# A state-space scan woven into a matmul stream: gate product in tile pieces, chunk splits moved to other rounds, DMA issues moved between queues

## The chip, the cores and the metric

The kernel runs on one core of one Trainium2 chip. The metric is the device time of one execution in microseconds (us), the median of three. Engines are named PE (matrix engine), DVE (vector), ACT (scalar), POOL (GpSimd) and SP (the queue that issues most transfers).

## What is computed

Two transformer-like blocks over 512 tokens of width 1024, in float32. The first block (retention, pooling, a convolutional feed-forward) and the last parts (attention, feed-forwards) are not touched. The change lies in the state-space mixer of the second block:

```python
u = (h @ w_in).reshape(bsz, seq, 64, 16)
bu = einsum('gnk,lgk->lgn', b, u)             # complex, 64 states per group
x  = associative_scan(combine, a, bu)         # x[l] = a * x[l-1] + bu[l]
y  = einsum('gkn,lgn->lgk', c, x) + d * u     # real part
z  = gelu(y)
val, gate = split(z @ w_glu, 2)
x  = x + val * sigmoid(gate)
```

## The kernel before

Every float32 product with a weight is made of three matmuls: the weight and the activation are each split into a high and a low part, and high*high, high*low and low*high are added in one PSUM bank. Weights come in **chunks** of 512 KB through a ring of six buffers (`RING`): SP issues the load of chunk n once chunk n-6 is used up, ACT writes the high part (L1161, `w_hi`), POOL the low part (L1012, `w_lo`), and PE waits for both in `take_chunk`. Where the weights have a gain, ACT first scales the chunk (L1156).

The stage of interest runs from about 621 to 749 us. PE first makes `u` for the first half of the columns (`("u", 0)`, L397 to L399), then for the second half tile by tile (`("u", 1)`, L428 to L430): four token tiles times four chunks, 16 slots of six matmuls. Beside these, 16 **rounds** of the scan run, one per batch of four groups. Rounds 0 to 5 sit in the slots that `round_in` names, rounds 6 to 15 follow. Round b is, on each engine in program order:

- PE: transpose the inputs of batch b+1 (`s5_states`, L712, bank `ut`), input product of batch b (`s5_inc`, L723, bank `sv`), output of batch b-2 (`s5_out`, L735 and L739, bank `y`), at some rounds a transpose back (`s5_turn_back`, L747, bank `zt`, where `back_in` says so), and from round 6 six matmuls of the gate product (`gate_rows`, L766 to L768).
- ACT: at the rounds of `made_in` the high part of one gate chunk (L1161); `u_t` of b+1 (L1383); the swapped state `sv_sw` (L1396, L1397); gelu of b-2 (L1391); the high part of what was turned back (L1170); the swapped `zs_sw` of b (L1405, L1406), which waits for DVE's `zs`.
- DVE: two products from the `sv` bank (L2079, L2080), `zc` of b-1 plus `zs_sw` (L2069, this frees PE's `s5_out(b-1)`), in rounds after those of `back_in` the low part (L1582, `a_lo`), then the subtraction with `sv_sw` (L2087), the scan (L2089), `zc` (L2097) and `zs` (L2098). The next round's ACT part hangs on this `zs`.
- POOL: the low parts of the gate chunks, and between them the decay tables `r_c` (L1001) that the scan reads. `decays_from` writes their order out: tables 0 to 5 before gate chunk 0's low part, 6 before chunk 1's, 7 to 10 before chunk 2's, 11 and 12 before chunk 3's, 13 to 15 after it. In this text gate chunks 0 to 3 are those of the first gate product `("glu_g", 0)`.

The gate product holds four PSUM banks; the other four go round among `ut`, `sv`, `y` and `zt`, so each bank is reused after four openings. A bank `zt` is free when DVE has made its low part.

The matrices of the scan (records, 544 KB and 256 KB per batch) were stored to DRAM earlier and are loaded again through four buffers (`RECS`): the first two by ACT, the next two and all later ones by SP between chunk loads, in the order that `next_records` writes out.

Of the kernel before, what the change touches and what calls it, by code (L numbers as in the profile page):

```python
# [85 lines left out]
def program(nc, x, w_in, w_pool, pool_scale, w_out, ln1_g, ln1_b, w_up, conv_w, conv_b, w_down, ln2_g, ln2_b,  # L86
# [7 lines left out]
    with ExitStack() as ctx:  # L94
# [226 lines left out]
        def _(pe):  # L321
# [431 lines left out]
            def gate_rows(k, tiles):  # L753

                j = k // 2
                if j not in gate_parts:
# [4 lines left out]
                wh, wl = gate_parts[j]
                pe.wait_ge(lo_ready, turned + k + 1)
                for t in tiles:
                    s = slice(t * P, t * P + P)
                    o = gate_banks[t]
                    pe.matmul(o, a_hi[:, k, s], wh[:, k % 2, :], start=(k == 0), stop=False)  # L766
                    pe.matmul(o, a_hi[:, k, s], wl[:, k % 2, :], start=False, stop=False)
                    m = pe.matmul(o, a_lo[:, k, s], wh[:, k % 2, :], start=False, stop=(k == KT - 1))  # L768
                    if k == KT - 1:
                        over = close_bank(("glu_g", 0, t), m)  # L770
                if k == KT - 1:
# [248 lines left out]
        def _(sp):  # L1020
# [58 lines left out]
            def stores_landed():  # L1079

                for i in range(2):
                    sp.wait_ge(st_out[i], 16 * (NB // 2))
                    sp.wait_ge(k_out[i], 16 * (NB // 2) * T)
                sp.wait_ge(e_out, 16 * NB)

            def load_attention_constants():

                for dst, src in ((hg[:, 0:ROPE], mla_k_rope_norm_2), (hg[:, ROPE:], mla_q_rope_norm_2[0]),
                                 (frq[:, :], c_freq)):
                    sp.dma_start(dst, src.partition_broadcast(P)).then_inc(m_in, 16)  # L1090
                for i, src in enumerate((mla_q_nope_norm_2[0], mla_k_nope_norm_2)):
                    sp.dma_start(gcol[0:NOPE, i:i + 1], src.rearrange("(e a) -> e a", a=1)).then_inc(m_in, 16)
                sp.dma_start(mask[:, :], c_mask).then_inc(m_in, 16)
                sp.dma_start(pos_i[:, :], positions_2[0].rearrange("(t p) -> p t", p=P)).then_inc(m_in, 16)
# [1221 lines left out]
```

## Time and profile before

| | |
|---|---|
| median of 3 runs | 1798.78 us (1798.54 to 1799.17) |
| the profiled execution | 1799.17 us, span 1797.3 us |
| PE busy | 1747.7 us, 97% of the span |
| DVE, ACT, POOL busy | 45%, 37%, 39% |
| stretch of the scan rounds | about 650 to 740 us |
| first matmul after the last gate matmul | 748.59 us |

The profile is of one execution. The timeline view gives instructions in order of time: start, duration, engine, line, operation, what is written from what, and in brackets the idle time of the engine before it with what ended it. The windows view gives busy time and granted clock of a stretch.

### The profile page before, as it was taken

Reading aid. Unit: us, or ns where it says so; the run is one execution under the profiler, and the core shown is the slowest. Engines: PE = TensorE matmul, PEld = TensorE weight load, DVE = VectorE, ACT = ScalarE, POOL = GpSimd, SP = SyncE. Lnnn points to the kernel's source line nnn. Section 1 sums busy time; section 2 is a strip of 40 time slices with the busy share of each in tenths; the row PEclk is TensorE's granted clock in tenths of the full one; section 3 lists DMA queues with packets and bytes.
Section 4 is the critical chain, followed back from the end, with each engine's and each line's share of the span. In section 5 each row is a group of like instructions: output and inputs, shape, how many; then the busy total and the mean of one; then the engine's idle time right before and its main releaser. Section 6 shows DMA issues by size and latency. Waiting matters only on the chain.

```text
span 1797.3 us, 22686 instructions
## 1 busy us (share of the span) xinstructions
PE 1747.7 (97%) x9006; PEld 1454.5 (81%) x9006; DVE 817.4 (45%) x1398; ACT 665.5 (37%) x1128; POOL 704.5 (39%) x331
## 2 busy tenths in 40 slices
PE   8999999899999899999999999999999999999999
PEld 6887977788788687789888888888888888888887
DVE  3876899779957637333211111138665311111111
ACT  3433234234244556524322313276654332122221
POOL 4432243534444232433453444433801345344442
PEclk9999999999999899999999999999999999999999
DMA  9422224353535367323333233222200233332332
GB/s 239 96 82 82 72 85 152 106 154 118 162 111 157 117 201 255 112 71 106 101 99 95 88 100 99 85 79 64 71 1 25 83 96 102 95 94 94 95 99 77
DMA packets 242280, 189.61 MB, mean 105 GB/s; under 512 B 41472, under 2 KB 199296, under 8 KB 242176
## 3 DMA queue, kind: packets, MB, share of 16 engines
q1 hardware_dynamic: 240304, 182.80, 34.1%
q10 hardware_dynamic: 1872, 5.37, 0.9%
q8 instruction: 72, 1.18, 0.3%
q14 instruction: 32, 0.26, 0.0%
HBM read 168.74 MB, written 19.40 MB: 105 GB/s over the span
## 4 chain that ended last, share of the span: by engine, by line
PE 82%; DVE 11%; ACT 3%; issue 2%; DMA 1%; POOL 1%; DVEq 0%; SPq 0%; ACTq 0%
PE ps L371 12%; PE ps L373 12%; PE ps L372 12%; PE ps L397 9%; PE ps L398 9%; PE ps L399 9%; PE ps L428 3%; PE ps L430 3%; PE ps L429 3%; PE ps L873 2%; PE ps L854 2%; PE ps L864 1%; DVE x_rows L1676 1%; ACT w_hi L1161 1%; PE ps L846 1%
## 5 line engine op out<-in xcount | busy, mean ns | idle before, releaser
L1012 POOL TENSOR_TENSOR w_lo<-w_raw,w_hi 128x1024 fp32r<-128x1024 f32 (+3 forms) x283 | 668.2, 2371 | 1032.2 <-ACT w_hi L1161 1032.1
L371 PE MATMUL ps<-a_hi,w_hi 128*128 128x512 f32 (+1 forms) x1184 | 442.5, 374 | 4.3 <-POOL w_lo L1012 4.3
L373 PE MATMUL ps<-a_hi,w_lo 128*128 128x512 f32 (+1 forms) x1184 | 440.5, 372 | 0.0
L372 PE MATMUL ps<-a_lo,w_hi 128*128 128x512 f32 (+1 forms) x1184 | 440.3, 372 | 0.0
L1161 ACT ACTIVATE w_hi<-w_raw 128x1024 fp32r<-128x1024 f32 (+3 forms) x283 | 284.9, 1018 | 214.8 <-DMA w_raw<-in_ffn_w_gate_up_dram 71.2
L371 PEld LDWEIGHTS ps<-a_hi,w_hi 128*128 128x128 f32 x1184 | 223.0, 188 | 45.5 <-issue 7.2
L373 PEld LDWEIGHTS ps<-a_hi,w_lo 128*128 128x128 f32 x1184 | 223.0, 188 | 38.9
L372 PEld LDWEIGHTS ps<-a_lo,w_hi 128*128 128x128 f32 x1184 | 223.1, 188 | 38.3
L2141 DVE TENSOR_TENSOR ev<-ps,xh 128x512 f32<-128x512 f32 x44 | 30.4, 691 | 411.9 <-PE ps L373 383.0
L397 PE MATMUL ps<-w_hi,h_hi 128*128 128x512 f32 x476 | 189.6, 398 | 8.7 <-DVE x_rows L1648 4.9
L398 PE MATMUL ps<-w_lo,h_hi 128*128 128x512 f32 x476 | 188.5, 396 | 0.0
L399 PE MATMUL ps<-w_hi,h_lo 128*128 128x512 f32 x476 | 188.4, 396 | 0.0
L1646 DVE TENSOR_TENSOR x_rows<-ps,x_rows 128x512 f32<-128x512 f32 x72 | 49.1, 690 | 224.8 <-PE ps L399 193.8
L1177 ACT ACTIVATE h_hi<-ev 128x512 fp32r<-128x512 f32 x66 | 41.5, 629 | 209.7 <-DVE ev L2141 195.5
L397 PEld LDWEIGHTS ps<-w_hi,h_hi 128*128 128x128 f32 x476 | 90.1, 189 | 32.0 <-issue 10.6
L397 PE MATMUL ps<-w_hi,a_hi 128*128 128x512 f32 (+1 forms) x288 | 113.2, 393 | 1.8 <-DVE a_lo L1582 1.8
L398 PE MATMUL ps<-w_lo,a_hi 128*128 128x512 f32 (+1 forms) x288 | 112.3, 390 | 0.0
L399 PE MATMUL ps<-w_hi,a_lo 128*128 128x512 f32 (+1 forms) x288 | 112.2, 390 | 0.0
L399 PEld LDWEIGHTS ps<-w_hi,h_lo 128*128 128x128 f32 x476 | 90.1, 189 | 21.2
L398 PEld LDWEIGHTS ps<-w_lo,h_hi 128*128 128x128 f32 x476 | 90.1, 189 | 20.7
L1260 ACT ACTIVATE xh<-ps 128x512 f32<-128x512 f32 x44 | 26.3, 598 | 166.2 <-PE ps L373 166.2
L428 PE MATMUL ps<-w_hi,a_hi 128*128 128x512 f32 (+2 forms) x208 | 77.4, 372 | 5.7 <-POOL w_lo L1012 2.4
(346 smaller groups left out, 2382.8 us busy)
## 6 DMA issues: line engine op xcount, KB each, us to landing
w_raw<-in_ffn_w_gate_up_dram SPq DMA_DIRECT2D x88, 512.0 KB, 3.8
w_raw<-in_w_up_dram SPq DMA_DIRECT2D x44, 512.0 KB, 3.9
w_raw<-in_ffn_w_down_dram SPq DMA_DIRECT2D x40, 512.0 KB, 3.7
w_raw<-in_w_in_dram SPq DMA_DIRECT2D x20, 512.0 KB, 4.3
w_raw<-in_w_down_dram SPq DMA_DIRECT2D x20, 512.0 KB, 4.3
s_records<-stage SPq DMA_DIRECT2D x16, 544.0 KB, 5.2
w_raw<-in_ssm_w_glu_dram SPq DMA_DIRECT2D x16, 512.0 KB, 3.7
rec<-s_records SPq DMA_DIRECT2D x14, 544.0 KB, 5.1
```

The costliest lines, as they stand in the source:

```text
L371: pe.matmul(bank, wh, xh_, start=first, stop=False)
L372: pe.matmul(bank, wh, xl_, start=False, stop=False)
L373: return pe.matmul(bank, wl, xh_, start=False, stop=last)
L397: pe.matmul(o, ah[:, k + kk, s], wh[:, kk, :], start=(n == 0 and kk == 0), stop=False)
L398: pe.matmul(o, ah[:, k + kk, s], wl[:, kk, :], start=False, stop=False)
L399: m = pe.matmul(o, al[:, k + kk, s], wh[:, kk, :], start=False, stop=end)
L428: pe.matmul(o, ah[:, k + kk, s], wh[:, kk, :], start=(k + kk == 0), stop=False)
L429: pe.matmul(o, ah[:, k + kk, s], wl[:, kk, :], start=False, stop=False)
L430: m = pe.matmul(o, al[:, k + kk, s], wh[:, kk, :], start=False, stop=end)
L1012: pool.tensor_tensor(w_lo[:, n % RING, 0:w], w_raw[:, n % RING, 0:w], w_hi[:, n % RING, 0:w].bitcast(F), ALU.subtract).then_inc(lo_made, 1)
L1161: act.activation(w_hi[:, n % RING, 0:w], w_raw[:, n % RING, 0:w], ACT.Copy).then_inc(hi_made, 1)
L1646: ins = v.tensor_tensor(o, b, o, ALU.add)
```

## The change

Four things are changed together.

- `gate_rows(k, tiles)`, one k-row at a time for a pair of tiles, becomes `gate_piece(j, tiles)`: both k-rows of one chunk for one tile. It starts at round 7 instead of 6, and waits once per chunk for the low part of the second k-row (for the last chunk, for the first and then the second). The order after round 15 is written anew.
- `back_in` has its first entry at round 5 instead of 4; `made_in` has the gate chunks at rounds 5, 6, 10 and 12 instead of 3, 7, 11 and 13. `decays_from` stays.
- `s5_states(0)` is issued before the first matmul of `("u", 1)` instead of inside it.
- ACT issues the loads of all four first records and of seven small attention constants; SP no longer issues these, and its later record loads follow one another in another order (`next_record`).

```diff
-        back_in = {4: 0, 6: 1, 8: 2, 10: 3, 12: 4, 14: 5}
+        back_in = {5: 0, 6: 1, 8: 2, 10: 3, 12: 4, 14: 5}
-        made_in = {3: 1, 7: 2, 11: 3, 13: 4}
+        made_in = {5: 1, 6: 2, 10: 3, 12: 4}
...
-            def gate_rows(k, tiles):
-
-                j = k // 2
+            def gate_piece(j, tiles):
+
                 if j not in gate_parts:
                     if not held:
                         gate_banks.extend(open_bank(("glu_g", 0, t)) for t in range(TT))
                         held.extend(bank_no["glu_g", 0, t] % 8 for t in range(TT))
+                    pe.wait_ge(lo_ready, turned + 2 * j + 2 - (j == TT - 1))
                     gate_parts[j] = take_chunk(rows_of(ssm_w_glu_2[0], 2 * j, 2, D, HALF), 2, HALF)
                 wh, wl = gate_parts[j]
-                pe.wait_ge(lo_ready, turned + k + 1)
-                for t in tiles:
-                    s = slice(t * P, t * P + P)
+
+                def row(t, kk):
+                    k, s = 2 * j + kk, slice(t * P, t * P + P)
                     o = gate_banks[t]
...
+                if j < TT - 1:
+                    for t in tiles:
+                        row(t, 0)
+                        m = row(t, 1)
+                    if tiles[-1] == TT - 1:
+                        chunk_over(m)
+                else:
+                    for t in tiles:
+                        row(t, 0)
+                    pe.wait_ge(lo_ready, turned + KT)
+                    for t in tiles:
+                        over = close_bank(("glu_g", 0, t), row(t, 1))
                     chunk_done.append(over)
...
-                if b_ >= 6:
-                    gate_rows((b_ - 6) // 2, (0, 1) if b_ % 2 == 0 else (2, 3))
+                if b_ >= 7:
+                    gate_piece((b_ - 7) // TT, [(b_ - 7) % TT])
+
+            s5_states(0)
 
             def beside_rows(t, n):
-                if TT * t + n == 1:
-                    s5_states(0)
...
             s5_out(NB - 2)
+            gate_piece(2, [1, 2])
+            s5_out(NB - 1)
             s5_turn_back(KT - 2)
-            gate_rows(KT - 3, range(TT))
-            s5_out(NB - 1)
+            gate_piece(2, [3])
             s5_turn_back(KT - 1)
-            gate_rows(KT - 2, range(TT))
-            gate_rows(KT - 1, range(TT))
+            gate_piece(3, range(TT))
...
-            def next_records(b_):
-                if b_ >= 2:
-                    sp.wait_ge(*closed(("y", b_ - 2)))
-                    load_out_part(sp, b_ - 2 + RECS)
-                if b_ + RECS < NB:
-                    sp.wait_ge(zs_ready, b_ + 1)
-                    load_state_part(sp, b_ + RECS)
+            def next_record(b_):
+                sp.wait_ge(zs_ready, b_ + 1)
+                load_state_part(sp, b_ + RECS)
+                sp.wait_ge(*closed(("y", b_)))
+                load_out_part(sp, b_ + RECS)
...
-                for later, rounds in ((5, range(0, 4)), (7, range(4, 5)), (9, range(5, 10)), (10, range(10, NB - 2))):
+                for later, records in ((RING - 1, range(0, 2)), (RING + 1, range(2, 3)), (RING + 3, range(3, NB - RECS))):
...
-            for b_ in range(2):
+            for b_ in range(RECS):
                 load_state_part(act, b_)
                 load_out_part(act, b_)
+            for dst, src in ((hg[:, 0:ROPE], mla_k_rope_norm_2), (hg[:, ROPE:], mla_q_rope_norm_2[0]),
+                             (frq[:, :], c_freq)):
+                act.dma_start(dst, src.partition_broadcast(P)).then_inc(m_in, 16)
...
             s5_gelu(NB - 2)
+            s5_gelu(NB - 1)
             split(("zt", KT - 2), *turned_back(KT - 2))
-            s5_gelu(NB - 1)
```

## Rows read from the trace of the kernel before

**Rows 1.** The page: span, and one line of its DMA issues.

```profile
span 1797.3 us, 22686 instructions
...
rec<-s_records SPq DMA_DIRECT2D x14, 544.0 KB, 5.1
```

**Rows 2.** Windows view: stretch, its length, busy PE, PEld, DVE, ACT, POOL; PEclk; DMA.

```profile
690.00:700.00 10.00, 8.69 (x78) 6.99 (x74) 7.45 (x14) 5.76 (x14) 3.88 (x4) 0.83 0.59 206
```

**Rows 3.** Timeline of PE: end of `("u", 0)`, and the first wait in `("u", 1)`.

```profile
640.40 0.39 PE L397 MATMUL ps<-w_hi,a_hi 128*128 128x512 f32 x1
...
645.84 0.39 PE L428 MATMUL ps<-w_hi,a_hi 128*128 128x512 f32 x1
...
652.59 0.47 PE L428 MATMUL ps<-w_hi,a_hi 128*128 128x512 f32 x1 [0.45 <-POOL w_lo L1012]
```

**Rows 4.** Timeline of ACT ahead of the rounds; ACTq is its queue of transfers.

```profile
628.33 0.45 ACTq L932 DMA_DIRECT2D rec<-s_records  x1
...
647.10 0.59 ACT L1374 ACTIVATE u_c<-ps 64x512 f32<-64x512 f32 x1 [1.04 <-DVE u_c L2058]
```

**Rows 5.** Timeline of DVE: the scans of rounds 4, 5 and 6.

```profile
678.18 0.69 DVE L2089 TENSOR_TENSOR_SCAN z<-r_c,z 128x256 f32<-128x256 f32 x1
...
684.70 0.69 DVE L2089 TENSOR_TENSOR_SCAN z<-r_c,z 128x256 f32<-128x256 f32 x1
...
689.06 0.69 DVE L2089 TENSOR_TENSOR_SCAN z<-r_c,z 128x256 f32<-128x256 f32 x1
```

**Rows 6.** Timeline of DVE in round 7, and the scans of rounds 8, 9 and 15.

```profile
691.59 0.42 DVE L2069 TENSOR_TENSOR zc<-zc,zs_sw 128x256 f32<-128x256 f32 x1
692.05 1.08 DVE L1582 TENSOR_TENSOR a_lo<-ps,a_hi 128x512 fp32r<-128x512 f32 x1
693.89 1.47 DVE L2087 TENSOR_TENSOR z<-z,sv_sw 128x256 f32<-128x256 f32 x1 [0.76 <-ACT sv_sw L1397]
695.71 0.78 DVE L2089 TENSOR_TENSOR_SCAN z<-r_c,z 128x256 f32<-128x256 f32 x1 [0.35 <-POOL r_c L1001]
...
700.23 0.69 DVE L2089 TENSOR_TENSOR_SCAN z<-r_c,z 128x256 f32<-128x256 f32 x1
...
704.72 0.69 DVE L2089 TENSOR_TENSOR_SCAN z<-r_c,z 128x256 f32<-128x256 f32 x1
...
735.85 0.69 DVE L2089 TENSOR_TENSOR_SCAN z<-r_c,z 128x256 f32<-128x256 f32 x1
```

**Rows 7.** Source view of L2087: instructions and durations in ns (min/median/max).

```profile
L2087 DVE TENSOR_TENSOR z<-z,sv_sw x16: 412/426/1472, 653.6 to 735.4; 128x256 f32<-128x256 f32 x16
```

**Rows 8.** Timeline of ACT and POOL in round 7.

```profile
691.58 1.06 ACT L1161 ACTIVATE w_hi<-w_raw 128x1024 fp32r<-128x1024 f32 x1
692.54 0.37 ACT L1383 ACTIVATE u_t<-ps 128x256 f32<-128x256 f32 x1
...
692.72 2.35 POOL L1012 TENSOR_TENSOR w_lo<-w_raw,w_hi 128x1024 fp32r<-128x1024 f32 x1 [13.14 <-ACT w_hi L1161]
```

**Rows 9.** Timeline of PE: start of round 8, then the tail after round 15.

```profile
693.19 0.46 PE L712 MATMUL ps<-ident,u_c 64*128 64x64 f32 x4 [1.31 <-DVE a_lo L1582]
693.57 1.10 PE L723 MATMUL ps<-u_t,rec 128*128 128x64 f32 x8
...
738.95 0.34 PE L735 MATMUL ps<-rec,u_t 128*64 128x64 f32 x4
...
740.58 0.66 PE L747 MATMUL ps<-ident,y_c 128*128 128x128 f32 x4 [0.48 <-ACT y_c L1391]
...
745.74 0.50 PE L766 MATMUL ps<-w_hi,a_hi 128*128 128x512 f32 x1 [1.60 <-DVE a_lo L1582]
...
748.59 0.39 PE L397 MATMUL ps<-w_hi,a_hi 128*128 128x512 f32 x1
```

**Rows 10.** Timeline of ACT in the tail.

```profile
740.54 2.96 ACT L1161 ACTIVATE w_hi<-w_raw 128x1024 fp32r<-128x1024 f32 x3
743.40 1.10 ACT L1170 ACTIVATE a_hi<-ps 128x512 fp32r<-128x512 f32 x1
```

More of the change, by code:

```diff
@@ L759, in gate_rows @@
                         held.extend(bank_no["glu_g", 0, t] % 8 for t in range(TT))
+                    pe.wait_ge(lo_ready, turned + 2 * j + 2 - (j == TT - 1))
                     gate_parts[j] = take_chunk(rows_of(ssm_w_glu_2[0], 2 * j, 2, D, HALF), 2, HALF)
                 wh, wl = gate_parts[j]
-                pe.wait_ge(lo_ready, turned + k + 1)
-                for t in tiles:
-                    s = slice(t * P, t * P + P)
+                def row(t, kk):
+                    k, s = 2 * j + kk, slice(t * P, t * P + P)
                     o = gate_banks[t]
[L766 to L771, printed above, removed]
+                    pe.matmul(o, a_hi[:, k, s], wh[:, kk, :], start=(k == 0), stop=False)
+                    pe.matmul(o, a_hi[:, k, s], wl[:, kk, :], start=False, stop=False)
+                    return pe.matmul(o, a_lo[:, k, s], wh[:, kk, :], start=False, stop=(k == KT - 1))
+                if j < TT - 1:
[10 more added lines that the diff above has]
+                        over = close_bank(("glu_g", 0, t), row(t, 1))
                     chunk_done.append(over)
-                elif k % 2 and tiles[-1] == TT - 1:
-                    chunk_over(m)
             def s5_round(b_):
@@ L1077, in store_batch @@
                                      e_t[:, :, GB * i:GB * i + GB, :]).then_inc(e_out, 16)
[L1079 to L1094, printed above, removed]
-            def next_records(b_):
-                if b_ >= 2:
-                    sp.wait_ge(*closed(("y", b_ - 2)))
-                    load_out_part(sp, b_ - 2 + RECS)
-                if b_ + RECS < NB:
-                    sp.wait_ge(zs_ready, b_ + 1)
-                    load_state_part(sp, b_ + RECS)
+            def next_record(b_):
[3 more added lines that the diff above has]
+                load_out_part(sp, b_ + RECS)
             for n, (src, kn, cn, _) in enumerate(chunk_src):
@@ L1112, in _ @@
                         store_batch(f)
-                if n == chunks_at[("u", 1, 0)] + 3:
-                    stores_landed()
-                    for b_ in range(2, RECS):
-                        load_state_part(sp, b_)
-                        load_out_part(sp, b_)
-                for later, rounds in ((5, range(0, 4)), (7, range(4, 5)), (9, range(5, 10)), (10, range(10, NB - 2))):
-                    if n == chunks_at[("u", 1, 0)] + later:
-                        for b_ in rounds:
-                            next_records(b_)
-                if n == chunks_at[("u", 1, 0)] + 13:
-                    load_attention_constants()
+                for later, records in ((RING - 1, range(0, 2)), (RING + 1, range(2, 3)), (RING + 3, range(3, NB - RECS))):
+                    if n == chunks_at[("u", 1, 0)] + later:
+                        for b_ in records:
+                            next_record(b_)
+            for i in range(2):
+                sp.wait_ge(st_out[i], 16 * (NB // 2))
+                sp.wait_ge(k_out[i], 16 * (NB // 2) * T)
+            sp.wait_ge(e_out, 16 * NB)
             for half in range(2):
@@ L1366, in _ @@
             act.wait_ge(e_out, 16 * NB)
-            for b_ in range(2):
+            for b_ in range(RECS):
                 load_state_part(act, b_)
                 load_out_part(act, b_)
+            for dst, src in ((hg[:, 0:ROPE], mla_k_rope_norm_2), (hg[:, ROPE:], mla_q_rope_norm_2[0]),
+                             (frq[:, :], c_freq)):
+                act.dma_start(dst, src.partition_broadcast(P)).then_inc(m_in, 16)
+            for i, src in enumerate((mla_q_nope_norm_2[0], mla_k_nope_norm_2)):
+                act.dma_start(gcol[0:NOPE, i:i + 1], src.rearrange("(e a) -> e a", a=1)).then_inc(m_in, 16)
+            act.dma_start(mask[:, :], c_mask).then_inc(m_in, 16)
+            act.dma_start(pos_i[:, :], positions_2[0].rearrange("(t p) -> p t", p=P)).then_inc(m_in, 16)
             def odd_rows(half, j):
```

## The prediction, made before the changed kernel was run

> **What bounds the kernel now.** I read the page first: PE is busy for 97% of the span [rows 1], so the question is only where PE waits, and whether a wait moves. The windows of ten us over the scan stage come next. In the worst of them PE is busy 8.69 of 10 us, and its granted clock is 0.83 [rows 2]. With the two levels of 2.4 and 1.2 GHz, a mean of 0.83 is (1 - 0.83) / 0.5 x 10 = 3.4 us at the lower one. Then I read the timelines engine by engine. The reader should see three things there.
>
> First, `("u", 1)` is set by PE itself: six matmuls a slot, 24 of them from 640.40 to 645.84, that is 0.227 us each, with one wait of 0.45 us at 652.59 [rows 3].
>
> Second, from round 5 on, the scan sets the pace. One scan follows the other by 4.36 us in round 6 (684.70 to 689.06) and by 4.49 us in round 9, both without a gate chunk, but by 6.65 us in round 7 (689.06 to 695.71) [rows 5, 6]. Round 7 has a chunk in front: ACT's `w_hi` comes 2.52 us after the scan of round 6, before `u_t` and `sv_sw`, for which DVE waits; POOL's `w_lo` starts 1.14 us after that and ends at 695.07 [rows 8]. DVE's subtraction starts at 693.89, takes 1.47 us instead of the usual 0.43, ends 0.29 us after POOL's pass, and the scan then waits 0.35 us for its table [rows 6, 7]. Rounds 7, 11 and 13 look so, 2.2 us longer than the others each.
>
> Third, after the scan of round 15 (735.85) a chain leads to the next product at 748.59, 12.74 us later: `y` of batch 15 at 738.95, gelu, three `w_hi` of the next product at 740.54, the last turned-back high part at 743.40, its low part, and PE at 745.74 after 1.60 us of waiting [rows 9, 10].
>
> **The change part by part.** Times below are before or after a scan; "scan 6" is that of round 6.
>
> *The early transposition.* `s5_states(0)` needs all four `u_c` copies. PE is free for it at 645.84, the last copy ends at 647.10 + 0.59 = 647.69 [rows 3, 4]. PE now stands still for 1.85 us with all of `("u", 1)` behind it. Later it had waited 0.45 us for the fourth chunk, whose chain starts at the same copy, and that wait goes. 1.85 - 0.45 = 1.4, less a switch of matmul shape that is saved: **+1.3 us** (bounds 1.0 and 1.9).
>
> *The transfers.* ACT issues six record loads more and seven constants, 13 x 0.45 = 5.9 us [rows 4]. What queues behind are `w_hi` of the chunks for `("u", 1)`, needed at 645.84 and later. The issues began before 628.33, so 19 of them end by 628.33 + 19 x 0.45 = 636.9; three chunks with 1.06 us for `w_hi` [rows 8] and, as my estimate, somewhat more for their scaling make 644, and the third is needed at 645.84 + 12 x 0.227 = 648.6 or later. Hidden: 0. Without that cover each further us would be on PE's path. On SP the constants were behind the last gate chunk and PE did not wait there: 0. The record loads change order: the state part for round b+4 is now issued after `y` of b-1, so in round b+1 instead of b. It is needed about two rounds later, some 9 us or more, and lands in 5.1 us [rows 1]. Taken as 0; the upper bound is one landing, 5.1 us.
>
> *Chunk 0 in round 5.* So far it lay in round 3 under PE's slots, free. Now its `w_hi` starts 2.52 us after scan 4, the POOL pass ends 2.52 + 1.14 + 2.35 = 6.01 us after it, and DVE's subtraction, stuck as in round 7, ends at 6.30, scan 5 at 6.34. Before, the distance was 6.52 (678.18 to 684.70, rounds paced by PE) [rows 5]. But in round 5 the add of `zs_sw` (L2069), like the subtraction a DVE instruction with both inputs in SBUF, also comes only after PE's `sv`, so during the POOL pass. If it is held as well, the subtraction follows with 0.43 and scan 5 is at 6.8. No row of before shows L2069 held. I take 6.8: **+0.3** (bounds -0.2 and +0.3). The transposition back that leaves round 4 gives PE 0.4 us, but ACT and DVE set this round: 0.
>
> The Trainium skill, "SBUF — State Buffer", section "SBUF: two separate sides", says that DVE with two SBUF inputs and a GpSimd instruction that reads SBUF exclude each other for the whole instruction. The 1.47 us of the subtraction agree. By this rule it is 6.8, by the add's own duration 6.34.
>
> *Chunks 1, 2 and 3 in rounds 6, 10 and 12.* These were in 7, 11 and 13. `decays_from` stays, so the tables behind each chunk are needed one round later, and the wait of 0.35 us for a table goes. The rest does not: `w_hi` still lies between `zs_sw` and `sv_sw`, and POOL's pass still meets the subtraction. A round with a chunk takes 6.65 - 0.31 = 6.34. In even rounds DVE has no low part to make meanwhile, but the POOL pass ends last anyway. Rounds 6 and 7: 6.34 + 4.49 against 4.36 + 6.65, -0.18. Three such pairs: **-0.5**. The removed wait is nearly all that is gained.
>
> *PE's gate pieces.* Here I see the new cost. The first piece of a chunk waits for the low part of the chunk's second k-row. In rounds 7, 11 and 15 that is the low part made in the same DVE round: it ends at 693.13, 4.1 us after the previous scan [rows 6]. PE used to do its six gate matmuls before that and then waited 1.31 us to open a bank on the same event [rows 9]. Now it waits first, and the matmuls (6 x 0.227 = 1.4, and 0.2 for switches) come behind, then `ut` (0.4) and `sv` (1.10). DVE's first product of round 8 can start 4.15 + 1.6 + 0.4 + 1.1 = 7.25 us after scan 6. ACT's `sv_sw` then starts at 7.7. By its own chain it would start 4.49 + 2.52 + 0.4 = 7.4 after. **+0.3** in round 8. In round 12 `w_hi` covers it: 0.
>
> *The tail.* In round 15 the piece of chunk 2 waits for the low part at scan 15 - 0.35. Behind it: six matmuls 1.36, `y` of 14 (740.10 - 738.95 = 1.15), twelve matmuls 2.72, switches 0.3. So `y` of 15 starts at scan 15 + 5.2, against 738.95 - 735.85 = 3.1 before [rows 6, 9]. It was ready at 3.1. Then ACT, which does gelu 15 first now, has the high part of `zt` 6 (1.1 us) between it and the three `w_hi`: 5.2 + 1.15 + 0.6 + 1.1 = 8.1, against 740.54 - 735.85 = 4.7 [rows 10]. Everything behind, up to 748.59, is as before: **+3.4**. The gate matmuls put ahead are work that must be done, but they filled PE's wait before; now PE waits elsewhere, ahead of round 15's piece and twice in the last chunk.
>
> *PE's clock.* A clock of 0.83 follows a PE idle of 1.31 us among thin matmuls [rows 2, 9]. The new idles are longer: in round 7 PE is done with `y` 5 about 6.0 us after scan 5 and waits until 6.34 + 4.15 = 10.5, some 4.5 us. In round 11 the same, in round 15 some 3.3. Half rate for 3.4 us costs 1.7 us of PE's work. Behind the first two waits PE is on the path: +1.7 in round 8, +1.0 in round 12 (1.7 + 0.3 less 1.0 us of `w_hi` in ACT's chain), +1.7 in the tail: **+4.4**. Bounds: 0, and in round 8 all 3.1 us of work behind the wait at half rate, +3.1.
>
> The Trainium skill, "TensorE: Matmul & The Clock Gate", section "HAM oscillation — how this bites in real kernels", warns that a loop with PE waits between short bursts runs each burst cold. The row at 0.83 agrees in kind.
>
> **Sum.** 1.3 + 0.3 - 0.5 + 0.3 + 3.4 = 4.8, with the clock 9.2. After 748.59 PE is filled again and I see nothing that takes the delay back. The profiled execution took 1799.17 us (span 1797.3): 1808.4. It lies 0.4 above the median of 1798.78, so 1808.0 us, 0.5% slower.
>
> **The rivals.** A measurement of this kernel tells 0.2% (3.6 us) from no change, not less.
>
> *The clock stays up.* The idles fall where little is left to lose, or the gate's six dense matmuls raise it at once. For it: after the 1.60 us before 745.74 twelve matmuls took 748.59 - 745.74 = 2.85 us, full rate [rows 9]. Then +4.8: 1803.6. Chance 0.20.
>
> *The moved chunk passes are hidden* (this ends at "not slower"). If PE, not the chain over ACT and DVE, set rounds 6, 10 and 12, `w_hi` and `w_lo` would lie in ACT's wait for `zs`. Price: 3 x 1.98 = 5.9 less, so +3.3, and with shorter waits no fall of the clock, -1.1. It decides from 5.6 us on. Against it: the subtraction in round 7 begins straight after ACT's chain and not after PE. Chance 0.20, at 1798 to 1802.
>
> *Hidden passes and a tail that fills.* If, besides, PE reaches round 15 so late that its wait there vanishes, the 3.4 are paid by work that had to be done anyway: -4.5, 1794. For it: removing three table waits and halving the gate's switches. Chance 0.09.
>
> *Records come late.* Round 6 or 7 waits for a state part behind two gate chunks in the queue: one landing more, 5.1: 1813. Chance 0.06.
>
> **How the numbers follow.** The forecast has 0.45. Slower: 0.45 + 0.20 + 0.06 = 0.71; within 0.2%: 0.20; faster: 0.09. The range reaches down to 1799, into the hidden case, and up to 1811.5 (the clock's 3.1 and the start's 1.9 in place of 1.7 and 1.3, with half a landing), leaving out faster, the ends of the hidden case and late records.
>
> **What would show it.** PE waits near 2 us on ACT's `u_c` before the first L712. L2087, and once L2069, at about 1.5 us or more beside POOL's pass in rounds 5, 6, 10 and 12; scans 6.3 us apart there and 4.5 in rounds 7, 11 and 13, with no wait on `r_c`. Gate matmuls of rounds 7, 11 and 15 waiting 3 us or more on `a_lo`. From scan 15 to the first matmul of `("glu_v", 0)` 16 to 18 us instead of 12.74. The forecast is wrong if scans of chunk rounds stay at 4.5 us, if the clock is at full rate behind the waits, or if a wait on `rec` appears.

## The result, and the profile after

The changed kernel is slower: median 1813.13 us (four runs, 1811.64 to 1814.99) against 1798.66 us for the kernel before (four runs, 1794.26 to 1799.17), a ratio of 1.0082 with a 95% interval of 1.0064 to 1.0099. Three more executions of it took 1810.29, 1810.93 and 1814.82 us. The direction was forecast; the median lies over the upper end of the range (1811.5). The profiled execution took 1814.82 us, its span is 1813.0 us, and it answers to the 1797.3 us of [rows 1]: 15.7 us more.

Line numbers have moved: L1161 is now L1147 (`w_hi`), L1170 L1156 (`a_hi`), L1374 L1367 (`u_c`), L1383 L1376 (`u_t`), L1582 L1575 (`a_lo`), L2069 L2062, L2079 L2072, L2087 L2080, L2089 L2082, L1437 L1430. The page of the changed kernel:

```profile
span 1813.0 us, 22687 instructions
...
PE 1755.1 (97%) x9006; PEld 1459.8 (81%) x9006; DVE 817.3 (45%) x1398; ACT 665.4 (37%) x1128; POOL 705.8 (39%) x331
```

PE's busy time rose by 7.4 us for the same count of matmuls: the same work at a lower clock. The other half is waiting. The view of PE's waits of the changed kernel gives what was waited for, us in total, times, and the longest:

```profile
PE ps L766 <- DVE a_lo L1575: 11.7, 5, 4.3
...
PE ps L712 <- ACT u_c L1367: 4.7, 1, 4.7
...
PE ps L723 <- DMA rec<-s_records: 2.2, 1, 2.2
```

PE's timeline of the changed kernel gives their places: before the rounds, in rounds 7, 11 and 15, and in the tail.

```profile
649.05 0.69 PE L712 MATMUL ps<-ident,u_c 64*128 64x64 f32 x4 [4.74 <-ACT u_c L1367]
650.26 0.63 PE L429 MATMUL ps<-w_lo,a_hi 128*128 128x512 f32 x1
...
694.03 1.10 PE L723 MATMUL ps<-u_t,rec 128*128 128x64 f32 x8 [2.20 <-DMA rec<-s_records]
...
700.97 0.77 PE L766 MATMUL ps<-w_hi,a_hi 128*128 128x512 f32 x1 [4.28 <-DVE a_lo L1575]
...
704.41 1.97 PE L723 MATMUL ps<-u_t,rec 128*128 128x64 f32 x8
...
725.53 0.50 PE L766 MATMUL ps<-w_hi,a_hi 128*128 128x512 f32 x1 [3.72 <-DVE a_lo L1575]
...
747.43 0.80 PE L766 MATMUL ps<-w_hi,a_hi 128*128 128x512 f32 x1 [2.25 <-DVE a_lo L1575]
...
755.77 0.34 PE L735 MATMUL ps<-rec,u_t 128*64 128x64 f32 x4
...
767.16 0.47 PE L397 MATMUL ps<-w_hi,a_hi 128*128 128x512 f32 x1 [0.32 <-ACT sig L1430]
```

The first matmul of `("glu_v", 0)` starts at 767.16 us, against 748.59 [rows 9]. All of the 15.7 us is lost by then and more: it stands 18.57 us later, though `("u", 0)` ended at 644.16, 1.68 us earlier than in [rows 3]. The 2.9 us that come back later are not the change's doing as far as the profiles show: after the stage the execution before has windows of ten us at 0.83, 0.93 and 0.90, that is 6.8 us at the lower clock or up to 3.4 us lost, and this one has 1.00 at the same work.

The windows of the changed kernel (columns as in [rows 2]) show where the clock fell:

```profile
640.00:650.00 10.00, 5.26 (x25) 4.06 (x24) 2.73 (x4) 9.88 (x15) 7.01 (x3) 0.89 0.77 273
650.00:660.00 10.00, 10.00 (x41) 7.85 (x41) 1.50 (x4) 2.87 (x6) 3.08 (x4) 0.77 0.01 2
690.00:700.00 10.00, 4.49 (x78) 3.85 (x74) 8.65 (x15) 6.21 (x14) 3.56 (x3) 0.78 0.93 329
700.00:710.00 10.00, 9.04 (x58) 7.55 (x59) 5.56 (x12) 3.74 (x9) 1.29 (x2) 0.54 0.24 62
```

In the fourth PE is busy for 9.04 us and gets through 58 matmuls; [rows 2] have 78 in 8.69 us. Shorter windows of the same trace tell when it fell:

```profile
692.00:695.00 3.00, 0.97 (x8) 0.97 (x8) 2.09 (x5) 2.88 (x7) 1.32 (x1) 1.00 1.03 389
697.00:701.00 4.00, 0.04 (x1) 0.07 (x1) 3.70 (x9) 2.43 (x6) 0.65 (x1) 0.50 0.79 228
701.00:709.00 8.00, 8.00 (x55) 6.61 (x55) 3.67 (x8) 2.43 (x6) 0.65 (x1) 0.50 0.11 40
```

The clock is still at its upper level at 695 us and already at the lower one when the wait of 4.28 us begins at 696.7. In windows of one us the low stretch runs from 695.5 to 709.2. What stands ahead of it is the other wait, 2.20 us before L723. The view names `rec` for that wait, but ACT's `u_t` for the same matmuls ends only 0.16 us before they start, because the chunk now split in round 6 stands ahead of it on ACT:

```profile
693.51 0.36 ACT L1376 ACTIVATE u_t<-ps 128x256 f32<-128x256 f32 x1
```

DVE's timeline of the changed kernel, rounds 5 to 8:

```profile
687.39 2.08 DVE L2062 TENSOR_TENSOR zc<-zc,zs_sw 128x256 f32<-128x256 f32 x1
...
690.03 0.69 DVE L2082 TENSOR_TENSOR_SCAN z<-r_c,z 128x256 f32<-128x256 f32 x1
...
694.86 1.48 DVE L2080 TENSOR_TENSOR z<-z,sv_sw 128x256 f32<-128x256 f32 x1 [0.75 <-ACT sv_sw L1390]
696.37 0.76 DVE L2082 TENSOR_TENSOR_SCAN z<-r_c,z 128x256 f32<-128x256 f32 x1
...
700.93 0.69 DVE L2082 TENSOR_TENSOR_SCAN z<-r_c,z 128x256 f32<-128x256 f32 x1
...
706.47 0.42 DVE L2072 TENSOR_TENSOR z<-ps,rec 128x256 f32<-128x256 f32 x1 [3.87 <-PE ps L723]
...
708.38 0.69 DVE L2082 TENSOR_TENSOR_SCAN z<-r_c,z 128x256 f32<-128x256 f32 x1
```

Round 5 holds L2062 for 2.08 us, round 6 (6.34 us long) holds the subtraction for 1.48 us and has no wait on `r_c`, round 7 takes 4.56 us. All that is as forecast. Round 8 takes 7.45 us: DVE stands idle for 3.87 us until PE's product is there.

### The profile page after: what moved, and what is told of

Its sections match the earlier page's. It is cut to its first block, busy times and chain, and to the rows that moved or that the text cites. A ratio compares the mean times of both kernels' runs of the same rounds, so it can differ in the third digit from the quotient of the medians.

```text
span 1813.0 us, 22687 instructions
## 1 busy us (share of the span) xinstructions
PE 1755.1 (97%) x9006; PEld 1459.8 (81%) x9006; DVE 817.3 (45%) x1398; ACT 665.4 (37%) x1128; POOL 705.8 (39%) x331
## 4 chain that ended last, share of the span: by engine, by line
PE 82%; DVE 11%; ACT 4%; issue 2%; DMA 1%; ACTq 1%; POOL 0%; DVEq 0%; SPq 0%
PE ps L371 12%; PE ps L373 12%; PE ps L372 12%; PE ps L397 9%; PE ps L398 9%; PE ps L399 9%; PE ps L428 3%; PE ps L429 3%; PE ps L430 3%; PE ps L881 2%; PE ps L862 2%; PE ps L872 1%; ACT w_hi L1147 1%; DVE x_rows L1669 1%; PE ps L854 1%
## 5 line engine op out<-in xcount | busy, mean ns | idle before, releaser
L1147 ACT ACTIVATE w_hi<-w_raw 128x1024 fp32r<-128x1024 f32 (+3 forms) x283 | 284.9, 1018 | 213.1 <-DMA w_raw<-in_ffn_w_gate_up_dram 70.9
```

What stands on the lines that cost most here:

```text
L1147: act.activation(w_hi[:, n % RING, 0:w], w_raw[:, n % RING, 0:w], ACT.Copy).then_inc(hi_made, 1)
```

## The experiments

Whole times answer badly here: the kernel before ran between 1788.7 and 1799.6 us in these sessions, with medians from 1794.85 to 1797.73, so 1 us can't be told. The traces can tell it. The ledger cuts the stage of each profiled execution at the scans: from the end of `("u", 0)` to scan 4, then from scan to scan, then from scan 15 to the first matmul of `("glu_v", 0)`. The line of the kernel before fits [rows 3, 5, 6, 9]; us throughout. Each line is one execution. Where an edit leaves a stretch alone, it repeats well: six kernels have 32.34 to 32.36 us up to scan 4.

| kernel | to scan 4 | round 5 | 6, 7 | 8, 9 | 10, 11 | 12, 13 | 14, 15 | tail | sum |
|---|---|---|---|---|---|---|---|---|---|
| before | 32.34 | 6.52 | 11.01 | 9.01 | 11.04 | 11.10 | 8.99 | 12.74 | 102.75 |
| after | 39.01 | 6.86 | 10.90 | 13.99 | 10.91 | 13.05 | 8.86 | 19.42 | 123.00 |
| add_early | 33.50 | 6.51 | 11.01 | 9.10 | 11.03 | 11.10 | 9.00 | 12.76 | 104.01 |
| add_queues | 32.52 | 6.52 | 11.03 | 9.02 | 11.03 | 11.10 | 8.99 | 12.78 | 102.99 |
| add_sched | 32.35 | 6.86 | 11.90 | 9.98 | 10.90 | 11.49 | 8.92 | 13.01 | 105.41 |
| add_gate | 32.35 | 6.52 | 11.02 | 11.80 | 11.04 | 11.10 | 8.95 | 18.22 | 111.00 |
| undo_queues | 33.49 | 6.87 | 10.89 | 13.82 | 10.90 | 13.02 | 8.87 | 16.71 | 114.57 |
| undo_early | 35.28 | 6.87 | 10.88 | 11.62 | 10.90 | 13.05 | 8.85 | 18.13 | 115.58 |
| undo_gate | 36.63 | 6.87 | 11.61 | 10.16 | 10.90 | 11.53 | 8.90 | 12.98 | 109.58 |
| fill_round7 | 33.49 | 6.87 | 10.90 | 10.05 | 10.89 | 13.80 | 8.87 | 17.92 | 112.79 |
| gelu_order | 32.36 | 6.51 | 11.01 | 9.02 | 11.02 | 11.10 | 8.97 | 13.92 | 103.91 |
| tail_first | 32.36 | 6.51 | 11.01 | 9.02 | 11.02 | 11.09 | 9.00 | 12.14 | 102.15 |
| decay_first | 32.36 | 6.51 | 10.77 | 9.01 | 10.77 | 10.84 | 8.98 | 12.79 | 102.03 |
| three_edits | 33.35 | 6.52 | 8.94 | 9.03 | 10.78 | 10.84 | 8.98 | 12.13 | 100.57 |

### One part alone, put into the kernel before

**add_early**: only the early transposition.

```diff
+            s5_states(0)
+
             def beside_rows(t, n):
-                if TT * t + n == 1:
-                    s5_states(0)
```

> The kernel before, with one edit of the change: the transposition of batch 0 is issued ahead of the second half of u. Theory (PE waits in order for the last u_c copy): one wait of PE on L712 of 1.9 us at about 646, the old wait of 0.45 us at the fourth chunk gone, no half rate behind it; first scan 1.2 to 1.8 us later, +1.3 us in all, 1800. Rival (the cost of the start lies only in the issue of transfers from ACT): 0, within 0.3 us. Rival (the wait alone lowers PE's clock): +3 us.

Measured: 1796.53 against 1797.73 us, ratio 0.9993 (0.9979 to 1.0007). The start grows by 1.16 us and PE waits 1.74 us, as its timeline in this kernel has it:

```profile
642.76 0.46 PE L712 MATMUL ps<-ident,u_c 64*128 64x64 f32 x4 [1.74 <-ACT u_c L1374]
```

The term of 1.3 us was right for this edit alone.

**add_queues**: only the transfers moved to ACT, and SP's new order.

```diff
-            for b_ in range(2):
+            for b_ in range(RECS):
                 load_state_part(act, b_)
                 load_out_part(act, b_)
+            for dst, src in ((hg[:, 0:ROPE], mla_k_rope_norm_2), (hg[:, ROPE:], mla_q_rope_norm_2[0]),
...
```

> The kernel before, with one edit of the change: ACT issues the 12 first record loads and the 7 constants, SP's later record loads in the new order. Theory (19 issues hold ACT for 13 us, some 0.7 us each and not 0.45): ACT idle of 12 us before its first scaling, u_c copies end 1.4 us later than before, the fourth chunk and with it PE 1.2 to 1.5 us later; +1 to +2 us in all, 1800.5. Rival (the transfers themselves come late, the records too): waits of PE on rec, +3 us or more. Rival of the prediction (hidden): 0.

Measured: 1799.50 against 1797.73 us, ratio 1.0003 (0.9990 to 1.0016); the start grows by 0.18 us. But ACT's timeline of this kernel shows that the issues are not cheap:

```profile
626.46 0.82 ACTq L927 DMA_DIRECT2D rec<-s_records  x2
...
636.75 0.81 ACTq L1355 DMA_DIRECT2D pos_i<-in_positions_dram  x1
637.61 1.34 ACT L1134 ACTIVATE w_raw<-w_raw,gains 128x512 f32<-128x512 f32 x2 [10.24 <-issue]
```

Nineteen issues took 11.1 us (626.46 to 637.56), not 8.6. The expectation of 1 to 2 us was wrong; the rival, hidden, is what this execution shows. PE has `("u", 1)` in front of the transposition here, and that work covers the wait. How thin this cover is, undo_early shows below.

**add_sched**: only `back_in` and `made_in`.

```diff
-        back_in = {4: 0, 6: 1, 8: 2, 10: 3, 12: 4, 14: 5}
+        back_in = {5: 0, 6: 1, 8: 2, 10: 3, 12: 4, 14: 5}
-        made_in = {3: 1, 7: 2, 11: 3, 13: 4}
+        made_in = {5: 1, 6: 2, 10: 3, 12: 4}
```

> The kernel before, with only the rounds of the gate chunks (5, 6, 10, 12) and of the first transposition back (5) of the change. Theory: intervals of scans 6.8 in round 5, 6.34 in rounds 6, 10 and 12, 4.5 in rounds 7, 11 and 13, L2062-like add held once to about 2 us; the stage 0 to +0.5 us, no wait on r_c; the time within 1 us of before. Rival (the table waits were the cost, 2.2 us each): 6 us less.

Measured: 1796.66 against 1794.85 us, ratio 1.0010 (0.9998 to 1.0022); the stage grows by 2.66 us. Round 5 has the 6.86 us and rounds 10 and 11 the 10.90 us of the changed kernel. The rest is that the old gate row of round 6 now waits 3.07 us for the low part of round 6, which the old table had made one round earlier; the clock is 0.72 from 690 to 700 us, and rounds 6 to 9 lose about 2 us. At most 0.5 us had been expected. These 2 us belong to the pairing of the new table with the old gate row of round 6, and the changed kernel, whose gate work starts at round 7, does not have them.

**add_gate**: only `gate_piece`, the order after round 15 and ACT's order of gelu.

```diff
+                    pe.wait_ge(lo_ready, turned + 2 * j + 2 - (j == TT - 1))
...
-                if b_ >= 6:
-                    gate_rows((b_ - 6) // 2, (0, 1) if b_ % 2 == 0 else (2, 3))
+                if b_ >= 7:
+                    gate_piece((b_ - 7) // TT, [(b_ - 7) % TT])
```

> The kernel before, with one edit of the change: gate_piece with its waits, its start at round 7, and the new order after round 15 on PE and ACT. Theory: PE waits 3 us or more on a_lo in rounds 7, 11 and 15 and its clock falls behind each; in rounds 8 and 12 most of it is hidden, because round 7 and 11 still are 6.65 us long (0 to 2 us in both together); from scan 15 to the first matmul of glu_v 0 it takes 16.1 us at full rate and 18 to 19.5 with half rate, instead of 12.7. +5 to +8 us, 1805. Rival (matmuls that must be done anyway, no loss): 0 to +1 us.

Measured: 1803.32 against 1797.73 us, ratio 1.0031 (1.0013 to 1.0049). The stage grows by 8.25 us: 2.79 in rounds 8 and 9, more than the expected 0 to 2, and 5.48 in the tail. PE waits 3.68 us in round 7 and 3.28 in round 15, but only 1.60 in round 11, where rounds 12 and 13 lose nothing. The windows of this kernel:

```profile
690.00:700.00 10.00, 7.14 (x50) 5.89 (x50) 6.72 (x12) 5.42 (x12) 3.89 (x4) 0.55 0.56 186
```

This is the dearest edit. The four alone sum to 1.26 + 0.24 + 2.66 + 8.25 = 12.4 us; together they cost 20.25. Some 8 us are interaction, or nearly 10 without the 2 us that only add_sched has, and 5.3 of these stand in the start (6.67 against 1.16 + 0.18 + 0.01 + 0.01).

### One part undone, in the changed kernel

**undo_queues**: the transfers back, the rest as changed.

```diff
-            for b_ in range(RECS):
+            for b_ in range(2):
                 load_state_part(act, b_)
                 load_out_part(act, b_)
...
```

> The changed kernel, with the record loads and constants back on SP in the old order. Theory (the start was mis-sized by the issue time on ACT, and the early transposition waits behind it): PE's wait on L712 falls from 4.7 to 1.9 us, with no half rate behind it, the rounds of u end 4.3 us earlier; the wait of 2.2 us on rec in round 7 goes without changing scan 8. -4 to -5 us against the changed kernel, 1809. Rival (the wait on rec is what lowers the clock in rounds 7 to 9): another 3 us less, 1806.

Measured: 1808.61 against 1797.73 us, ratio 1.0051 (1.0034 to 1.0068). The start is back at 33.49 us and PE's wait before L712 at 1.74 us; no window around 650 us is below 1.00. So 5.5 of the start's 6.7 us need the transfers. Rounds 8 and 9 stay (13.82 against 13.99 us), though no wait is put down to `rec` any more. But PE stands at the same place just as long, 2.15 us before the input product of round 7. So `rec` was not what held it, nor what lengthened rounds 8 and 9. The tail is 16.71 us, and here the clock is 1.00 throughout it:

```profile
740.00:750.00 10.00, 7.75 (x89) 6.21 (x90) 4.32 (x9) 3.75 (x10) 0.00 (x0) 1.00 0.10 35
750.00:760.00 10.00, 8.26 (x36) 6.00 (x35) 2.19 (x2) 8.77 (x11) 7.12 (x3) 1.00 0.34 107
```

**undo_early**: `s5_states(0)` back inside `("u", 1)`.

```diff
-            s5_states(0)
-
             def beside_rows(t, n):
+                if TT * t + n == 1:
+                    s5_states(0)
```

> The changed kernel, with the transposition of batch 0 back in its slot. Theory (the early transposition is what turns ACT's 13 us of issues into a stop of PE, and that stop halves the clock): no wait on L712 over 0.5 us, no half rate at 650, first scan about 1 us later than before instead of 5.6; 5 us less than the changed kernel, 1808, although this edit alone costs only 1 us and the queues alone 0.2. Rival (the two edits add up): 1.3 us less, 1812.

Measured: 1809.14 against 1794.85 us, ratio 1.0074 (1.0049 to 1.0098). The start is 35.28 us: 3.7 less than in the changed kernel, but 2.8 more than in add_queues. ACT's issues took 12.3 us here, PE waits 0.98 us for `w_lo` of the next chunk, and the clock is 0.83 from 650 to 660 us, that is 3.4 us at half rate or 1.7 us lost. The wait on L712 is gone as expected (0.16 us), but the low clock and a start 2.9 us longer than in the kernel before were not expected. The issues end 6.0 us before PE is through with `("u", 0)`, in add_queues 7.1 us before it. This 1.2 us less is the only difference found in this stretch. So the transfers cost 0.2 us in one trace and 2.9 us in another, both without the early transposition.

**undo_gate**: the gate product by k-rows again, with the old order after round 15.

```diff
-                if b_ >= 7:
-                    gate_piece((b_ - 7) // TT, [(b_ - 7) % TT])
+                if b_ >= 6:
+                    gate_rows((b_ - 6) // 2, (0, 1) if b_ % 2 == 0 else (2, 3))
```

> The changed kernel, with the gate matmuls as before: k-row by k-row from round 6 on, old order after round 15 on PE and ACT. Theory (the gate pieces cost 8 us of the stage by themselves and more through the clock): scans 8 and 9 follow after 4.5 us each, the tail from scan 15 to glu_v 0 is 12.7 us again; what stays is the start (+5.6), round 5 (+0.3) and the pairs (-0.1 to -0.2 each). 11 to 12 us less than the changed kernel, 1802. Rival (chunks in even rounds cost as well): rounds 6, 10 and 12 stay at 6.3 but 7, 11 and 13 do not fall to 4.6.

Measured: 1802.21 against 1794.85 us, ratio 1.0037 (1.0021 to 1.0053). Tail 12.98 us, rounds 8 and 9 10.16, rounds 12 and 13 11.53. With the gate pieces go 6.4 us of the tail, 3.8 of rounds 8 and 9, and 1.5 of rounds 12 and 13. But rounds 6 and 7 grow by 0.7 us to 11.61: this kernel has the pairing of add_sched again, with a wait of 2.98 us at the gate row of round 6, so the 3.8 us are a net figure. The wait before L712 is 3.27 us.

### Is it the clock?

**fill_round7**: undo_queues with eight matmuls more. PE runs them into a free gate bank, before it waits for the low part in round 7; the first real piece overwrites what they leave.

```diff
+                if b_ == 7:
...
+                    pe.wait_ge(lo_ready, turned + 1)
+                    for _ in range(8):
+                        pe.matmul(gate_banks[3], a_hi[:, 0, 0:P], a_hi[:, 0, :], start=True, stop=True)
```

> The changed kernel with loads back on SP (undo_queues), and eight more matmuls of 512 columns on PE in round 7, in the wait ahead of the first gate piece; they write a gate bank that the first real matmul starts anew, so the output is the same. Theory (half rate behind the wait is what makes rounds 8 and 9 long, 7.4 and 6.4 us): PE is at full rate from the gate piece on, round 8 takes 4.8 us and round 9 4.5, 4 to 4.5 us less in the stage than undo_queues. Rival (order of the work, not clock): rounds 8 and 9 stay as long, or grow by the eight matmuls.

Measured: 1806.33 against 1794.85 us, ratio 1.0063 (1.0041 to 1.0086). The wait for the low part ends no earlier, but it is filled, and what follows is faster. The same two groups of matmuls, first in undo_queues:

```profile
695.95 0.77 PE L766 MATMUL ps<-w_hi,a_hi 128*128 128x512 f32 x1 [4.12 <-DVE a_lo L1590]
...
699.39 1.97 PE L723 MATMUL ps<-u_t,rec 128*128 128x64 f32 x8
```

then in fill_round7:

```profile
692.00 3.58 PE L797 MATMUL ps<-a_hi 128*128 128x512 f32 x8
...
696.50 0.50 PE L766 MATMUL ps<-w_hi,a_hi 128*128 128x512 f32 x1 [0.91 <-DVE a_lo L1596]
...
698.48 1.11 PE L723 MATMUL ps<-u_t,rec 128*128 128x64 f32 x8
```

From the first gate matmul to the input product 3.44 us become 1.98, and the product itself 1.97 become 1.11. The windows say the same, first undo_queues ahead of and in the wait:

```profile
686.00:690.00 4.00, 1.85 (x16) 1.51 (x15) 3.02 (x7) 3.19 (x7) 1.30 (x1) 1.00 0.95 320
692.00:695.00 3.00, 0.00 (x0) 0.00 (x0) 2.73 (x7) 1.75 (x5) 0.65 (x1) 0.50 0.25 70
```

then fill_round7 in the filled wait and behind it:

```profile
692.00:695.00 3.00, 3.00 (x9) 2.43 (x8) 2.73 (x7) 0.98 (x4) 1.11 (x2) 0.50 0.19 73
696.50:705.00 8.50, 8.50 (x104) 7.08 (x104) 5.83 (x14) 5.21 (x12) 1.30 (x2) 1.00 0.70 223
```

In both the clock has fallen before the gate's wait, behind the wait of 2.15 us ahead of L723. The eight matmuls themselves run at the lower level, 3.58 us or 0.45 each against 0.227 in [rows 3]. Left idle, PE stays at the lower level for 13.7 us; filled, for 3.4 us. Rounds 8 and 9 take 10.05 us instead of 13.82: 3.8 us of the 4.8 lost there were the clock's. Round 8 takes 4.77 us as expected, round 9 5.28 and not 4.5. The Trainium skill, "TensorE: Matmul & The Clock Gate", section "HAM oscillation — how this bites in real kernels", warns of bursts that run cold between waits; this pair of traces agrees, and has its price.

The stage gains less, 1.8 us and not the expected 4 to 4.5: low stretches now stand later (0.79 and 0.70 from 710 to 730 us, 0.85 in the tail), and 2 us go back. By whole times this kernel can't be told from undo_queues (ratios 1.0063 and 1.0051 to the kernel before, with intervals that overlap).

### The tail and the tables

**gelu_order**: the kernel before, with only the gelu of batch 15 ahead of the high part of `zt` 6 on ACT, and PE's two outputs before both transposes back.

```diff
             s5_out(NB - 2)
-            s5_turn_back(KT - 2)
             gate_rows(KT - 3, range(TT))
             s5_out(NB - 1)
+            s5_turn_back(KT - 2)
             s5_turn_back(KT - 1)
...
             s5_gelu(NB - 2)
+            s5_gelu(NB - 1)
             split(("zt", KT - 2), *turned_back(KT - 2))
-            s5_gelu(NB - 1)
```

> The kernel before; of the change only the order after round 15 on ACT (gelu of batch 15 ahead of the high part of the last but one tile) and of the two transpositions back on PE, without the gate pieces that the change puts ahead of the last output. Theory (in the changed tail two things lie in ACT's chain: the last output 2.8 us later behind gate matmuls on PE, and one high part of 1.1 us ahead of the three w_hi): tail from scan 15 to glu_v 0 13.8 to 14.1 us instead of 12.74, +1.2 us. Rival (the whole 4 us come from the order on ACT): 16 us or more.

Measured: 1796.62 against 1797.68 us, ratio 1.0002 (0.9990 to 1.0014), tail 13.92 us. Of the 4.0 us by which the tail grows at full clock (16.71 less 12.74), 1.2 are this order. The other 2.8 are left for the gate pieces ahead of the last output; that is a difference, and twelve matmuls at 0.227 us fit it.

**tail_first**: the kernel before; ACT makes the last turned-back high part ahead of the three `w_hi` of the next product.

```diff
-            limit[0] = 10 ** 6
             load_gain(1, ffn_norm_2[0])
             split(("zt", KT - 1), *turned_back(KT - 1))
+            limit[0] = 10 ** 6
```

> The kernel before, with one line moved: ACT takes the high part of the last turned-back tile before it makes the three w_hi of the next product, not after. Theory (these 2.96 us stand in the chain behind scan 15): PE no longer waits 1.60 us on a_lo before its last twelve gate matmuls, tail 11.0 to 11.2 us instead of 12.74, POOL's first low part still in time. -1.6 us. Rival (the next product then waits for POOL): tail unchanged, the wait on w_lo at the first matmul of glu_v 0 instead.

Measured: 1795.14 against 1796.99 us, ratio 0.9991 (0.9978 to 1.0003), tail 12.14 us: 0.6 less and not 1.6. PE's wait of 1.60 us for `a_lo` [rows 9] is gone, but another takes its place, for the sigmoid that is now behind the `w_hi` and a table load of 1.28 us:

```profile
747.01 0.47 PE L397 MATMUL ps<-w_hi,a_hi 128*128 128x512 f32 x1 [1.14 <-ACT sig L1437]
```

**decay_first**: the kernel before, with one table more made ahead of the low part of chunks 1, 2 and 3.

```diff
-            decays_from = {0: range(0, 6), 1: range(6, 7), 2: range(7, 11), 3: range(11, 13), 4: range(13, NB)}
+            decays_from = {0: range(0, 6), 1: range(6, 8), 2: range(8, 12), 3: range(12, 14), 4: range(14, NB)}
```

> The kernel before, with one decay table more made ahead of each gate chunk's low part (tables 7, 11, 13 move ahead). Theory (only 0.35 us of the 2.2 us of a chunk round is the table wait, the rest is w_hi and DVE's held subtraction): rounds 7, 11 and 13 take 6.3 instead of 6.65 us, no wait on r_c; -1 us in the stage. Rival (the table wait is the cost): 4.5 us each, -6.5 us.

Measured: 1796.11 against 1796.99 us, ratio 0.9996 (0.9984 to 1.0008). Rounds 7, 11 and 13 take 6.32 to 6.33 us, and each pair gains 0.24 to 0.27 us. In this kernel's DVE timeline the hold stays:

```profile
692.57 1.46 DVE L2087 TENSOR_TENSOR z<-z,sv_sw 128x256 f32<-128x256 f32 x1 [0.75 <-ACT sv_sw L1397]
694.07 0.77 DVE L2089 TENSOR_TENSOR_SCAN z<-r_c,z 128x256 f32<-128x256 f32 x1
```

So a chunk round costs 6.32 us without any wait for a table, and the prediction priced the moved chunks with 6.34.

This trace also shows that a short idle does not always lower the clock. PE waits 1.32 us ahead of L712 in round 8, as in [rows 9], and 1.44 us two rounds later, and the clock is 1.00 in every window from 640 to 770 us; in the kernel before it was 0.83 in two of them.

**three_edits**: the kernel before, with tail_first, tables 6 to 11 ahead of chunk 2, and gate chunk 1 in round 4, where PE sets the pace, instead of round 7.

```diff
-        made_in = {3: 1, 7: 2, 11: 3, 13: 4}
+        made_in = {3: 1, 4: 2, 11: 3, 13: 4}
...
-            decays_from = {0: range(0, 6), 1: range(6, 7), 2: range(7, 11), 3: range(11, 13), 4: range(13, NB)}
+            decays_from = {0: range(0, 6), 2: range(6, 12), 3: range(12, 14), 4: range(14, NB)}
```

> The kernel before, with three edits: the last high part first as in tail_first, the tables ahead as in decay_first, and gate chunk 1 made in round 4 (made_in 3, 4, 11, 13), where PE's slots set the pace. Theory: round 7 takes 4.5 us, round 4 or 5 grows by 0.3 us because the add is held by POOL's pass, rounds 11 and 13 take 6.3, tail 11.1; the stage 4 us shorter, 0.2% less time. Rival (work moved ahead of round 7 only moves the wait to PE's bank): round 8 grows by what round 7 loses.

Measured: 1790.97 against 1796.99 us, ratio 0.9978 (0.9965 to 0.9992), the one version whose interval lies clear of the kernel before on the fast side. Rounds 6 and 7 take 8.94 us, 2.1 less; round 4 pays 1.0 of it instead of the expected 0.3, because `w_hi` delays ACT's copy:

```profile
670.20 0.46 PE L712 MATMUL ps<-ident,u_c 64*128 64x64 f32 x4 [0.93 <-ACT u_c L1374]
```

The stage gains 2.2 us, not 4. The median gains 6.0; I can account for the 2.2 only, and the clock from 690 to 700 us is 1.00 in its profile against 0.83 [rows 2].

## Why the prediction was wrong in size

**The step that failed: "ACT issues six record loads more and seven constants, 13 x 0.45 = 5.9 us ... Hidden: 0."** The price of 0.45 us was read from the few issues of the kernel before [rows 4]. ACT's timeline of the changed kernel:

```profile
626.87 0.82 ACTq L935 DMA_DIRECT2D rec<-s_records  x2
...
635.63 1.46 ACTq L1359 DMA_DIRECT2D frq<-in_c_freq_dram  x1
...
639.36 0.45 ACTq L1363 DMA_DIRECT2D pos_i<-in_positions_dram  x1
639.86 1.34 ACT L1142 ACTIVATE w_raw<-w_raw,gains 128x512 f32<-128x512 f32 x2 [12.09 <-issue]
...
646.95 2.05 ACT L1367 ACTIVATE u_c<-ps 64x512 f32<-64x512 f32 x4
```

Nineteen issues took 12.9 us (626.87 to 639.81), 0.68 each; the first six still 0.46, the thirteen behind them 0.78. They end 2.9 us later than the 636.9 of the forecast. Worse was the list of what queues behind them. I named the `w_hi` of the coming chunks, but behind those stand the four `u_c` copies (to 649.00, where those of [rows 4] end at 647.69), and the early transposition makes all of PE's work wait for exactly these. "Without that cover each further us would be on PE's path" was written in the prediction; the cover was taken away by the part priced one paragraph earlier. PE waits 4.74 us instead of 0.45, and then runs slowly: (1 - 0.77) / 0.5 x 10 = 4.6 us at the lower clock in the window from 650 us, 2.3 us lost. 4.3 + 2.3 = 6.6, against 6.67 in the ledger and 1.3 forecast. The 2.3 are a little low: the clock fell before PE's wait was over (0.89 from 640 to 650 us), and the transposition at 649.05 already took 0.69 us instead of 0.46. Of the 2.9 us by which the wait is longer than the forecast 1.85, 1.3 are the later `u_c` (649.00 against 647.69); the other 1.7 are that PE came to this point 1.68 us earlier in this execution and only stands longer. undo_gate, with the same transfers and transposition, has 3.27 us of waiting and +4.3. Each edit alone costs 1.2 and 0.2 us (add_early, add_queues), and 5.5 of the 6.7 go with the transfers (undo_queues). The full loss was seen only with both edits, but undo_early shows 2.9 us with the transfers and without the early transposition: the traces fit a loss wherever the issues end too late for the cover, and their length differed from trace to trace.

The rate of 0.227 us a matmul, which the prediction gives to `("u", 1)`, was read from the last 24 matmuls of `("u", 0)` [rows 3]; those of `("u", 1)` start 0.23 us apart too, so nothing hangs on it.

**Round 5: right.** 6.86 us against 6.8. L2062 took 2.08 us instead of 0.42. The rule of the Trainium skill, "SBUF — State Buffer", section "SBUF: two separate sides", by which 6.8 was chosen over 6.34, holds here.

**Chunks 1 to 3: right.** 10.90 and 10.91 us against 11.01 and 11.04, forecast -0.18 a pair. The rival of hidden passes is out: chunk rounds take 6.32 to 6.35 us wherever they are put among rounds 6 to 13 (add_sched, decay_first), as long as PE is not late; round 12 of the changed kernel, where it is, takes 6.86. Where PE sets the pace, the chunk cost 1.0 us instead of 1.9 (three_edits, round 4).

**Gate pieces and the clock in rounds 8 and 9: mechanism right in part, size short by 3.** Forecast +0.3 and +1.7, measured +4.98. The step that was mis-sized is "Half rate for 3.4 us costs 1.7 us": the two windows at 0.78 and 0.54 hold (0.22 + 0.46) / 0.5 x 10 = 13.6 us at the lower clock, 4.28 of it in the wait itself. The forecast also had a single wait in round 7. There are two, and the clock falls behind the first, 2.20 us ahead of L723, which no term of the sum has: the chunk in round 6 puts `w_hi` ahead of ACT's `u_t`, and PE has no gate matmuls in round 6 any more. add_gate, without that chunk, waits 1.04 us there and loses 2.79 us in rounds 8 and 9. That the second wait keeps the clock down is shown by fill_round7. That the first brings it down is what the order of the rows says; no run removed it alone. The upper bound of 3.1 us was set for round 8 alone. Round 9 follows late too: 6.54 us against 4.49. With full clock it is still 5.28 us (fill_round7), because when PE is late DVE's low part stands between the first product and the scan in odd rounds: 2.7 us from one to the other, where round 8 has 1.9 (706.47 to 708.38). I had not counted this.

**Rounds 12 and 13:** forecast +1.0 less 0.18, measured +1.95. The same two causes show in the trace: the clock is at its lower level from 726.2 to 733.1, behind the wait of 3.72 us, and in round 13 DVE's first product starts at 736.19, 2.7 us ahead of the scan. No run tells the two apart here.

**The tail: order right, clock short.** At full clock (undo_queues) `y` of 15 starts 5.3 us after scan 15 (forecast 5.2), the three `w_hi` at 8.07 (8.1), and the tail is 16.71 (16.1). In the changed kernel `y` of 15 starts at 755.77, 8.03 after the scan at 747.74, 2.7 us later by the clock instead of the 1.7 forecast, and everything behind takes as long as in undo_queues (11.39 and 11.38 us).

**Late records:** a wait put down to `rec` appeared in round 7, which the prediction had named as a sign that it is wrong. It was no such sign: undo_queues waits as long there without it, and scan 7 came 4.56 us after scan 6. That this rival had 1813 us, the time that was measured, is luck.

**Sum.** Forecast 9.2 us for the stage, measured 20.2 (less the 1.7 that PE was early and the 2.9 that came back later, the 15.7 of the span): start +5.4, rounds 8 and 9 +3.0, rounds 12 and 13 +1.1, tail +1.6 (19.42 - 12.74 = 6.7 against 5.1). The upper end of the range was added up wrongly, too: 1808.0 with 1.4 for the clock, 0.6 for the start and half a landing, 2.6, is 1812.6 and not 1811.5; the measured 1813.13 lies above both. What stays open: why ACT's issues took 11.1 us in one kernel and 12.3 to 12.9 in others, and what moves the clock stretches outside the stage (the 1.7 ahead of it, the 2.9 behind).

## What to carry to other kernels

Price edits of one change together: list what stands on each in-order queue after all of them, and check whether a cover that one edit counts on is what another removes. A wait placed ahead of work that used to fill it can cost more than its length, since the matmuls behind it may run at the lower clock, as here; give PE work that is ready before the wait, and leave the wait where less hangs on it. When a clock has fallen, look with short windows at what stands ahead of the fall: it need not be the longest wait. Where one engine's pass holds another's instruction, move it to a stretch that a third engine bounds.

## What the runs showed that I had not expected

Transfers issued back to back from ACT: the first six in 2.75 us, later single ones 0.45 to 1.46 us, and 19 of them stopped ACT's compute for 11.1 to 12.9 us. Eight matmuls without use, put into a wait of 4.1 us, made the two rounds behind it 3.8 us shorter, though they ran at the lower clock themselves. The lower clock moves: taken away in one place, it appeared in fill_round7 at 710 to 730 us, and cut the gain.
